# Two expert tables: 32 tokens instead of 16 gather their experts' rows beside the dense work

## What is computed

```python
def chunk(xc):
    q = (xc @ wq).reshape(PEER_CHUNK, PEER_HEADS, 2, PEER_HALF)
    s = jnp.einsum('chpd,hpkd->chpk', q, subkeys)
    ...                                        # top 16 of 16 x 16 sums of two top-16 lists
    g = jax.nn.softmax(cs, axis=-1)            # 8 heads x 16 experts a token
    ug = jnp.take(u_table, eidx, axis=0)
    vg = jnp.take(v_table, eidx, axis=0)
    hid = jnp.einsum('cd,chkd->chk', xc, ug)
    a = jax.nn.gelu(hid, approximate=False) * g
    return jnp.einsum('chk,chkd->cd', a, vg)
```

## Time and profile before

| | |
|---|---|
| median of 3 runs | 2464.5 us |
| span of the profiled execution, first to last instruction | 2460.4 us |
| what lies around the span, median less span | 4.1 us |
| U table on TensorE | 402.7 to 987.7 us |
| V table on TensorE | 987.9 to about 1504 us |
| granted TensorE clock, mean | 0.997 |

### The profile page before, as it was taken

How to read it: one execution, slowest core, us unless ns; L and a number is a source line. 1 busy time by engine, 2 the same in 40 slices (tenths; PEclk the granted TensorE clock), 3 DMA queues, 4 the chain that set the end, 5 groups by cost and what they waited for, 6 DMA issues and landing times.

```text
span 2460.4 us, 35608 instructions
## 1 busy us (share of the span) xinstructions
PE 2413.0 (98%) x13533; PEld 2191.6 (89%) x13533; DVE 1823.9 (74%) x3411; ACT 1199.0 (49%) x2113; POOL 567.1 (23%) x372
## 2 busy tenths in 40 slices
PE   8999999999999999999999999999999999999998
PEld 7788888899999998999999998888788888888887
DVE  7876678999999886899999998777785326433323
ACT  6555466378778886433333345444422224322222
POOL 3222064133333552455545520000000000000000
PEclk9999999999999999999999999999999999999999
DMA  4211345599999999999999982322574222223331
GB/s 172 70 54 51 121 156 167 177 327 324 343 325 319 396 407 360 406 411 412 412 411 408 409 309 78 107 78 86 171 254 153 91 98 95 94 90 99 103 101 37
DMA packets 193114, 533.89 MB, mean 217 GB/s; under 512 B 16712, under 2 KB 65896, under 8 KB 190768
## 3 DMA queue, kind: packets, MB, share of 16 engines
q1 hardware_dynamic: 151472, 380.60, 43.2%
q0 software_dynamic: 41472, 151.01, 16.1%
HBM read 480.09 MB, written 51.46 MB: 216 GB/s over the span
## 4 chain that ended last, share of the span: by engine, by line
PE 84%; DVE 9%; DMA 3%; ACT 2%; issue 2%; POOL 0%; DVEq 0%; SPq 0%; ACTq 0%
PE P L1349 26%; PE P L1351 26%; PE P L1350 26%; DMA GB<-un,SI 3%; DVE wl L1824 2%; PE P L1714 1%; PE P L1356 1%; DVE D L1824 1%; DVE T L1827 0%; ACT wh L2527 0%; DVE GB L2160 0%; PE P L1629 0%; PE P L1628 0%; PE P L1627 0%; PE P L1606 0%
## 5 line engine op out<-in xcount | busy, mean ns | idle before, releaser
L1349 PE MATMUL P<-XH,wh 128*128 128x512 f32 (+2 forms) x2272 | 835.3, 368 | 9.7 <-DVE wl L1824 9.7
L1351 PE MATMUL P<-XH,wl 128*128 128x512 f32 (+2 forms) x2272 | 817.7, 360 | 0.0
L1350 PE MATMUL P<-XL,wh 128*128 128x512 f32 (+2 forms) x2272 | 817.4, 360 | 0.0
L2527 ACT ACTIVATE wh<-raw 128x1024 fp32r<-128x1024 f32 x458 | 482.3, 1056 | 396.2 <-PE P L1351 396.2
L1824 DVE TENSOR_TENSOR wl<-raw,wh 128x1024 fp32r<-128x1024 f32 x422 | 512.2, 1222 | 74.6 <-ACT wh L2527 72.1
L1349 PEld LDWEIGHTS P<-XH,wh 128*128 128x128 f32 x2272 | 428.2, 188 | 56.7 <-DVE wl L1824 13.2
L1351 PEld LDWEIGHTS P<-XH,wl 128*128 128x128 f32 x2272 | 427.8, 188 | 47.6
L1350 PEld LDWEIGHTS P<-XL,wh 128*128 128x128 f32 x2272 | 428.6, 189 | 42.6 <-issue 1.9
L1349 PE MATMUL P<-AH,wh 128*128 128x368 f32 (+1 forms) x1024 | 337.5, 330 | 1.1 <-DVE AL L1824 1.1
L1350 PE MATMUL P<-AL,wh 128*128 128x368 f32 (+1 forms) x1024 | 336.7, 329 | 0.0
L1351 PE MATMUL P<-AH,wl 128*128 128x368 f32 (+1 forms) x1024 | 336.7, 329 | 0.0
(11 more groups left out here) (345 smaller groups left out, 3389.0 us busy)
## 6 DMA issues: line engine op xcount, KB each, us to landing
raw<-wts SPq DMA_DIRECT2D x211, 512.0 KB
raw<-ut SPq DMA_DIRECT2D x128, 512.0 KB
raw<-vt SPq DMA_DIRECT2D x128, 512.0 KB
hdram<-HID SPq DMA_DIRECT2D x64, 384.0 KB
HI<-hdram SPq DMA_DIRECT2D x32, 768.0 KB
gdram<-GS SPq DMA_DIRECT2D x23, 1024.0 KB
GI<-gdram SPq DMA_DIRECT2D x16, 1472.0 KB, 11.4
AWC<-adat SPq DMA_DIRECT2D x64, 256.0 KB, 5.3
```

Source lines behind the costliest of these rows:

```text
L1349: e.matmul(bank, wh[:, w], H, start=start, stop=False)
L1350: e.matmul(bank, wh[:, w], L, start=False, stop=False)
L1351: return e.matmul(bank, wl[:, w], H, start=False, stop=stop)
L2527: return e.activation(dst, src, ACT.Copy)
```

## The change

`NX` becomes 32. From it follow: 32 gathers and 32 weighted sums of the first kind instead of 16 on each table (`NDOT` 148, `NROW` 172), `STEP0` 8 (the grids start with n = 8, 88 of them instead of 92), `GROUP0` 2, `PARTS` 4, and matmuls of 352 columns in both tables, save in V's first unit. The numbers by which side work is dealt are others: routing 4.1 a step instead of 3.4 and 4.0, dots 1.35 and 2.05 a step instead of 1.2 and 1.8, a weighted sum 5.3 credits instead of 5.8. Four small tiles move in on-chip memory, and the count of grid stores is written for any `GROUP0`.

```diff
--- before.py
+++ after.py
@@ -23,7 +23,7 @@
 NRAW = 6
 
 LATE = 12
-NX = 16
+NX = 32
 PARTS = 128 // NX
 AMONG = 44
 NDOT = 128 - LATE + NX
@@ -546,7 +546,7 @@
             if STEP0 <= n - 1 < 96:
                 yield ("weigh", n - 1)
             yield 1.6 if n % 2 and n > STEP0 + 2 else 3.1
-            due += 3.4 if n < 32 else 4.0
+            due += 4.1
             while due > 0:
                 piece = next(more, None)
                 if piece is None:
@@ -554,7 +554,7 @@
                 yield piece
                 if not isinstance(piece, tuple):
                     due -= piece
-            dots_due += 1.2 if n < 30 else 1.2 if n < 62 else 1.8
+            dots_due += 1.35 if n < 62 else 2.05
             yield from some(int(dots_due))
             dots_due -= int(dots_due)
         yield from some(NDOT)
@@ -603,7 +603,7 @@
                 yield ("axpy", s - LATE - NX)
             if s == LATE - 1:
                 yield ("dots_end", 1)
-            yield 5.8
+            yield 5.3
         yield from prepare()
 
     for s in range(5):
@@ -847,10 +847,10 @@
         gmod = at("gmod", 58.5625, [128, 16], F32)
         st = at("st", 58.625, [128, 64], F32)
         SIX = at("SIX", 57.53125, [128, NX], U32)
-        GX = at("GX", 57.59375, [128, NX], F32)
-        HSX = at("HSX", 57.65625, [128, NX], F32)
-        TOKEN = at("TOKEN", 58.90625, [128, NX], F32)
-        invf = at("invf", 58.875, [128, 1], F32)
+        GX = at("GX", 104.125, [128, NX], F32)
+        HSX = at("HSX", 104, [128, NX], F32)
+        TOKEN = at("TOKEN", 58.875, [128, NX], F32)
+        invf = at("invf", 58.28125, [128, 1], F32)
         SI = at("SI", 59, [128, 128], U32)
         HS = at("HS", 59.5, [128, 128], F32)
         XH = at("XH", 60, [128, 8, T], F32R)
@@ -1145,7 +1145,7 @@
             return sum(not high_on_act(i) for i in range(STEP0, n + 1))
 
         def grid_writes(g):
-            return g // 2 + 1 - (GROUP0 > 0 and g % 2 == 0)
+            return g // 2 + 1 - (GROUP0 + 1 - g % 2) // 2
 
         def rows_done(r):
```

## The result

The changed kernel takes 2483.3 us, the median of 4 runs (2482.6 to 2483.8), against 2464.2 us of the kernel before on the same chip. The ratio is 1.0080, 95% interval 1.0068 to 1.0093: 0.8% slower. Forecast were 2464 us and a range of 2440 to 2480, so the result lies outside it.

What follows compares the result with a forecast made beforehand. TensorE was taken as fullest, with VectorE at 93 to 95% and, in V, the DMAs nearly full too. Terms -6 + 3 + 12 - 7 - 2.5 = -0.5 us on 2460.4, plus 4.1 for the median: 2464 us, range 2440 to 2480.

Steps and rivals of the forecast that it cites:

- the fourth: V's first 112 units: limits of 430 (TensorE), 436 (VectorE) and 437 us (DMAs), taken as 441, -7 us.
- First: U's first 88 units, up to 796.5 us: VectorE's share rises to 97%, 388 us, -6 us.
- Second: U from 796.5 to 954.9 us, 32 units: DMAs move 63.65 MB at 395 GB/s, +3 us.
- Third: Where the tables meet, 954.9 to 987.9 us: more gathers, then a TensorE wait of 8 us; +12 us.
- the chain from grid store to `AL`: Where the tables meet: last grids' store, gates' load, product and low part take 24.6 us; TensorE waits 8 us.
- The term of the DMAs: V's first 112 units: 13.5 MB per eight units at 411 GB/s take 32.9 us; fourteen such are 460 us.
- the credit of 18 us for full buffers: V starts with six unit loads and eight gathers already buffered, 7.3 MB, cutting the DMAs' 455 us to 437.
- a first eight with 7 gathers: V's first eight units have only 7 gathers, taking 6 us off the DMAs' 460 us.
- the rotation: Rival: six gather buffers set V when gathers take over 13 us; units over 4.05 us, total 2478 us; chance 0.25.
- Fifth: V's last 16 units, after gathers end: TensorE saves 2.6 us, taken as -2.5 us.
- the first rival: DMAs give more than they were asked for; V's first 112 units take 436 us, total 2444 us; chance 0.24.
- The others for "right": Signs: 160 ns matmuls, about 8 us TensorE idle before V ended by `AL`, VectorE over 97% busy in V.

Runs made afterwards that it cites:

- half rows in V: Changed kernel with V's gathers in units 8 to 127 fetching half of each row, sums reading it twice: 2463.8 us, ratio 0.9996.
- 16 tokens with the new numbers: Kernel before (NX = 16, 368 columns) with only the changed kernel's numbers for dealing side work: 2487.8 us, ratio 1.0097.
- 32 tokens and the old numbers: Changed kernel (NX = 32, 352 columns) with side work dealt by the numbers of the kernel before: 2498.4 us, ratio 1.0140.

## Why the prediction was wrong

The step that failed is the fourth, V's first 112 units: it took 18 us off the DMAs' time for full buffers and 6 us for the first eight units, and the runs show neither. It alone holds 18.8 of the 21.3 us between the forecast and the table's sum. In the prediction's order:

- *"A matmul takes 160.0 ns and a unit of 24 takes 3.84 us instead of 4.00 ... 40.8 us."* A line through 368 and 512 columns gave a number that the chip doesn't take in this kernel: its matmuls start every 158.3 or every 166.7 ns. Even the kernel with half rows in V, without a wait behind the first eight units, took 444.1 us for V main, not 430. In V this term didn't decide the result, since the DMAs are slower than either rate.
- *First, U to unit 88, -6 us.* Measured -3.8. VectorE was named as the limit of all 88 units; it holds TensorE back only in the first 25, where the faster rate is partly eaten by 2.7 us more of waits for `wl`. Behind them TensorE's own rate, mostly 166.7 ns, is the limit, and 10% less work on VectorE gains 0.5 us over all 88. Of the 3.8 us, 2 are the four grids left out.
- *Second, +3.* Measured +1.5, at 397 GB/s with 62 of the list's 64 gathers. The size was right; see the third for what it is made of.
- *Third, +12.* Measured +9.9, but not by the chain from grid store to `AL`. TensorE had no gap before V, and 3.71 us before U's last units, behind the row of dots. The prediction had this row done "before the gates land"; both ended at 984 us. Taking load off both ends left U end at 203.0 us. Together with the second stretch, 15 us were forecast and 11.4 measured, what 5.9 MB more of gathers would take. But 16 tokens with the new numbers lose 10.8 us there with no more bytes, so how the loss divides between bytes and dealing stays open.
- *Fourth, -7.* Measured +11.8. The term of the DMAs was right: 32.9 us for eight units, 14 such are 460 us, and V main is 461.6, in which 189.6 MB were moved at 411 GB/s; 14 x 13.5 MB are 189. What failed is the credit of 18 us for full buffers. Eight gathers of it weren't there: V's first gather is issued at 995.94 us, 0.43 us into V. The six loads of the table were there and were not used up: in the middle of V a unit's load still lands 18 to 23 us before its first matmul, while most gathers land less than 2 us before their sum. So VectorE, holding a sum for a gather, stops what stands behind it, `AL`, and TensorE waits. The 6 us taken off for a first eight with 7 gathers weren't there either: units 1 to 9 took 32.0 us at 414 GB/s, and 11 gathers were issued in them. By its own sum this step without the credit gives 455, +7, and all steps together 2478, the rival whose price came nearest. Its condition was met, a gather takes 14.1 us, over its 13; but two more buffers changed nothing, so its mechanism, the rotation, was refuted. One run leaves a part open: with 32 tokens and the old numbers TensorE did not stand in V main, and while units 65 to 121 passed the DMAs moved 87.4 MB, where the list asks for 7 x 12.97 = 90.8. So about 3.4 MB came out of full buffers there (an estimate from these rows), and such a credit can exist at another pace.
- *Fifth, -2.5.* Measured +1.4, with some gathers still under way (share 0.67 instead of 0.56).
- The Trainium skill's 425 GB/s ("DMA: Bandwidth & Descriptors", section "Bandwidth"): over 394 us of V no run went above 411, with more buffers, less work on VectorE or fewer bytes, and no eight units were above 415. For gathers and loads mixed as here, 411 is the limit, and the first rival falls.
- Of the signs named beforehand, VectorE's waits for `GV` came. The others for "right" did not: 160 ns, a wait for `AL` before V, VectorE over 97% busy (91%). V's units took 4.12 us each, the sign named for the rotation. It shows that gathers land late, and can't tell too few buffers from full DMAs.

The balance of the kernel before could have told it: TensorE at 32.0 us for eight units and DMAs at 13.1 MB, 31.9 us at 411 GB/s. Any edit that adds bytes to V is paid in full.

## What to carry to other kernels

Where two resources are both full, price an added load by the bytes of each step of work, and subtract a credit for full buffers only if the trace shows those buffers filled ahead and run empty at the end. Don't extrapolate an instruction's interval to a size that the trace doesn't have; measure it, in a stretch that runs without waits. Deal side work into the stretch whose queues have room (here ahead of unit 88, at 330 GB/s), and look for bytes that carry nothing. After a change of pace, count what the list leaves over for its end.

## What the runs showed of the hardware that was not expected

The interval between matmuls of 352 columns had two steady values, 166.7 and 158.3 ns (400 and 380 cycles at 2.4 GHz), with the same instruction in the same kernel. 352 columns that begin at 16 instead of 32 took 160.0 ns, and 360 columns take as long as 368.

After a wait of 3.7 us where the tables meet, TensorE's granted clock falls to 0.50, which is 1.2 GHz. (Between 972 and 974 us it was busy for only 0.16 us, and the clock stayed at 1.00.) The busy time of the changed kernel in windows of 2 us:

```profile
984.00:986.00 2.00, 0.00 (x0) 0.00 (x0) 1.51 (x5) 1.81 (x5) 0.00 (x0) 1.00 0.41 99
986.00:988.00 2.00, 1.79 (x7) 1.79 (x8) 2.00 (x3) 2.00 (x3) 0.00 (x0) 0.68 0.97 372
988.00:990.00 2.00, 2.00 (x8) 2.00 (x8) 0.50 (x3) 0.15 (x1) 0.00 (x0) 0.50 0.93 381
990.00:992.00 2.00, 2.00 (x13) 2.00 (x13) 0.00 (x0) 0.09 (x1) 0.00 (x0) 0.96 1.04 388
```

About 12 matmuls start every 293 ns there instead of 158 to 167, so the wait of 3.7 us costs another 1.6. In the kernel before TensorE did not wait there and its clock stayed at 1.00.
